# Both products of a feed forward by seven products of half-sized blocks in place of eight

## The reference

```python
h2 = rms_norm(x, norm2[l])
x = x + jnp.square(jax.nn.relu(h2 @ w_up[l])) @ w_down[l]
return rms_norm(x, final_norm)
```

## Time and profile before

| | |
|---|---|
| median of 3 runs | 1938.89 us (1938.49 to 1940.59) |
| the profiled execution | 1938.64 us; span 1936.6 us |
| busy: PE, DVE, ACT, POOL | 1904.5, 968.0, 778.3, 92.8 us |
| granted clock of TensorE, mean | 1.000 |
| chain that ended last | PE 89%, DVE 6%, ACT 3%, issue 2% |
| moved by DMA | 129.29 MB |

### The profile page before, as it was taken

How to read it: one execution, slowest core, us unless ns; L and a number is a source line. 1 busy time by engine, 2 the same in 40 slices (tenths; PEclk the granted TensorE clock), 3 DMA queues, 4 the chain that set the end, 5 groups by cost and what they waited for, 6 DMA issues and landing times.

```text
span 1936.6 us, 23640 instructions
## 1 busy us (share of the span) xinstructions
PE 1904.5 (98%) x9297; PEld 1577.2 (81%) x9297; DVE 968.0 (50%) x2069; ACT 778.3 (40%) x1482; POOL 92.8 (5%) x165
## 2 busy tenths in 40 slices
PE   8999999999999999999999999999999999999998
PEld 6888888868888888887888888888888888888887
DVE  5788764546676666665321244433343433333234
ACT  5566333347777777776211132312030312212022
POOL 4111001100000000000000000000000000000000
PEclk9999999999999999999999999999999999999999
DMA  5410124322232212222321141212020211112002
GB/s 169 115 34 28 55 87 152 102 67 66 61 77 72 74 52 64 74 61 59 95 54 44 55 159 48 66 44 66 22 76 23 75 33 55 55 33 66 22 22 87
DMA packets 132479, 129.29 MB, mean 67 GB/s; under 512 B 7233, under 2 KB 112265, under 8 KB 132370
## 3 DMA queue, kind: packets, MB, share of 16 engines
q1 hardware_dynamic: 126482, 115.18, 19.7%
q0 software_dynamic: 5888, 12.62, 2.9%
...
## 4 chain that ended last, share of the span: by engine, by line
PE 89%; DVE 6%; ACT 3%; issue 2%; DMA 0%; POOL 0%; DVEq 0%; POOLq 0%; SPq 0%; ACTq 0%
PE b L86 85%; PE b L89 4%; DVE Wf L108 1%; DVE Wr L97 1%; ACT Wf L94 1%; DVE Xr L97 1%; ACT Wf L93 1%; DVE Wf L97 1%; ACT Wr L93 1%; DVE ring L97 1%; ACT Xr L93 0%; DVE Yf L105 0%; DVE Wf L101 0%; DVE Yr L105 0%; ACT ring L93 0%
## 5 line engine op out<-in xcount | busy, mean ns | idle before, releaser
L86 PE MATMUL b<-Yr,ring 128*128 128x512 f32 x1920 | 507.9, 400 | 1.1 <-DVE Xr L97 1.1
L86 PE MATMUL b<-Xr,ring 128*128 128x512 f32 x1872 | 452.7, 393 | 3.3 <-DVE Xr L97 1.5
L86 PEld LDWEIGHTS b<-Xr,ring 128*128 128x128 f32 x1872 | 345.6, 189 | 70.9 <-issue 4.2
L86 PEld LDWEIGHTS b<-Yr,ring 128*128 128x128 f32 x1920 | 340.1, 189 | 56.0 <-DVE Xr L97 1.5
L86 PE MATMUL b<-Xr,Yr 128*128 128x512 f32 x1104 | 254.0, 390 | 0.0
L86 PEld LDWEIGHTS b<-Xr,Yr 128*128 128x128 f32 x1104 | 206.8, 188 | 42.8
L86 PE MATMUL b<-Yr 128*128 128x512 f32 (+2 forms) x1040 | 236.1, 375 | 0.0
L86 PEld LDWEIGHTS b<-Yr 128*128 128x128 f32 x1040 | 190.7, 188 | 38.1
L97 DVE TENSOR_TENSOR Wf<-Wf,b 128x512 f32<-128x512 f32 x144 | 92.6, 684 | 237.7 <-PE b L86 237.7
L93 ACT ACTIVATE Wf<-b 128x512 f32<-128x512 f32 (+3 forms) x215 | 106.2, 494 | 229.1 <-PE b L86 225.5
L94 ACT ACTIVATE Wf<-Wf,st 128x640 f32<-128x640 f32 (+3 forms) x192 | 125.2, 652 | 162.1 <-DVE st L112 58.8
...
## 6 DMA issues: line engine op xcount, KB each, us to landing
stage<-in_w_in_dram SPq DMA_DIRECT2D x58, 512.0 KB, 4.0
stage<-in_w_up_dram SPq DMA_DIRECT2D x32, 512.0 KB, 4.0
stage<-in_w_down_dram SPq DMA_DIRECT2D x32, 512.0 KB, 3.5
stage<-in_w_out_dram SPq DMA_DIRECT2D x16, 512.0 KB, 3.5
...
Yf<-in_x_dram SPq DMA_DIRECT2D x8, 512.0 KB, 6.4
Wf<-in_x_dram SPq DMA_DIRECT2D x8, 512.0 KB, 4.4
scratch_x<-Wf SPq DMA_DIRECT2D x8, 512.0 KB, 2.7
```

The costliest lines, as they stand in the source:

```text
L86: return self.send(lambda e: e.matmul(o, w, a, start=start, stop=stop))
```

## The change

Both products are made by the seven-product scheme (Winograd's form of Strassen's). With a 2 x 2 split of each operand, blocks of the weights or of the hidden values are combined into S1 to S4, blocks of the other operand into T1 to T4, and seven products P1 to P7 of half-sized blocks take the place of eight; their sums give the four quarters of the result.

**Up phase.** All of the up product comes first. A pair i of 16 has two groups of 128 columns of `w_up`. For each pair VectorE forms S1, S2 (`s12f`) and S4, S3 (`s43f`); ScalarE and VectorE split these and the plain blocks into high and low parts (`a`, `s12`, `s43`, `a22`). T1, T2, T3 of the activations are made tile by tile from the transposes of tiles 4 to 7 (`tile`, `lows`), T4 later in one piece (`T4f`, `T4`). A product is 12 matmuls. P6, P7 and P4 continue to sum on P1's bank and P3 on P5's (`matmul_onto`, L90 in the changed kernel); copies of the sums between are `r1`, `z5`, `u2`. ScalarE makes relu and square of the four results, VectorE their combinations (`US`, `U4`), and seven kinds of block are written to a new tensor `u_d` in HBM. The table UP_ORDER gives the order in every queue.

**Down phase.** 28 steps n: 4 chunks c of 1024 hidden channels by 7 products. A step is 48 matmuls. A share of `u_d` is loaded for each; ScalarE and VectorE split it (S) and the weights' block (T); GpSimd forms T1 to T4 of the weights. VectorE adds the banks to seven sums in SBUF (in the first chunk ScalarE copies four of them). In the last chunk the seven sums are combined, by GpSimd in pieces of 128 x 2048 and by VectorE, and the final norm follows. The rows of x wait in HBM during the up phase.

```diff
@@ tensor_program @@
-             (7, 3): turn_h3(5)})
+             (7, 3): turn_h3(5), (7, 6): turn_h3(6)})
-    for c in range(8):
-...
+    def seventh(kind, i, room, k0, acts, b, fresh):
+        w = room.rearrange("p (l k c) -> p l k c", l=2, c=P)
+        for k in range(4):
+            for n, (lw, la) in enumerate(((0, 0), (0, 1), (1, 0))):
+                last = k == 3 and n == 2
+                if fresh:
+                    sent = pe.matmul(m.banks[b], w[:, lw, k0 + k, :], acts[:, k, la, :], k == 0 and n == 0, last)
+                else:
+                    sent = pe.matmul_onto(m.banks[b], w[:, lw, k0 + k, :], acts[:, k, la, :], last)
+        sent.then_inc(m.p_dense, (kind, i))
+    for kind, i in UP_ORDER:
+        p, q, r = P_BANKS[i % 3], Q_BANKS[i % 2], R_BANKS[i % 2]
+        if kind == "tile" and i == 7:
+            turn_rows("f", 7, m.ht3[1], TURN_BANKS)
+        elif kind == "P1":
+            pe.wait_ge(*at["low", "a", i])
+            pe.wait_ge(*at["ht", "f", 3, 1])
+            pe.wait_ge(*at[freed[p]])
+            seventh("P1", i, m.room_a[i % 2], 0, m.B11, p, True)
+...
+        elif kind == "P4":
+            pe.wait_ge(*at["low", "a22", i])
+            pe.wait_ge(*at["T4 low"])
+            pe.wait_ge(*at["C22", i])
+            seventh("P4", i, m.room_a22, 0, m.T4, p, False)
+            freed[p] = ("C21", i)
+    for n in range(28):
+        pe.wait_ge(*at["low S", n])
+        pe.wait_ge(*at["low T", n])
+        for t in range(4):
+            b = LAST_BANKS[(4 * n + t) % 8]
+            pe.wait_ge(*at[freed[b]])
+            for k in range(4):
+                for i, (ls, lt) in enumerate(((0, 0), (0, 1), (1, 0))):
+                    sent = pe.matmul(m.banks[b], m.room_s[n % 2][:, k, ls, block(t)], m.room_t[n % 2][:, k, lt, :],
+                                     k == 0 and i == 0, k == 3 and i == 2)
+            sent.then_inc(m.p_dense, ("back", n, t))
+            note.bank["back", n, t] = b
@@ the tables of the order @@
+    out = [("post", 7), ("tile", 6), ("row", 7), ("P1", 0), ("lows", 6), ("P2", 0), ("C11", 0), ("P1", 1), ("tile", 7),
+           ("lows", 7), ("P2", 1), ("P5", 0), ("s43f", 0), ("s43", 0), ("P6", 0), ("a22", 0), ("P3", 0), ("s12f", 1),
+           ("s12", 1), ("P7", 0), ("US", 0), ("C11", 1), ("P5", 1), ("s43f", 1), ("T4f", 0), ("P6", 1), ("a", 2),
+           ("P1", 2), ("s43", 1), ("P3", 1), ("T4", 0), ("P4", 0), ("U4", 0), ("s12f", 2), ("a22", 1), ("P7", 1),
+           ("s12", 2)]
+    for i in range(2, PAIRS):
+        if i > 2:
+            out += [("P1", i), ("P7", i - 1)]
+        out += [("P5", i), ("s43f", i), ("US", i - 1), ("P2", i), ("C11", i), ("s43", i), ("P4", i - 1), ("U4", i - 1)]
+        if i < PAIRS - 1:
+            out += [("a", i + 1), ("P6", i), ("s12f", i + 1), ("P3", i), ("s12", i + 1), ("a22", i)]
+        else:
+            out += [("P6", i), ("P3", i), ("a22", i), ("prep", 0), ("P7", i), ("US", i), ("P4", i), ("U4", i)]
+    return out
+...
+DOWN_ORDER = ("P1", "P5", "P2", "P3", "P6", "P7", "P4")
+STORED = ("A11", "A12", "A22", "S1", "S2", "S3", "S4")
+SHARE_OF = {"P1": "A11", "P2": "A12", "P3": "S4", "P4": "A22", "P5": "S1", "P6": "S2", "P7": "S3"}
+P_BANKS, Q_BANKS, R_BANKS = (0, 4, 5), (1, 7), (2, 3)
+LAST_BANKS = (6, 4, 5, 1, 7, 2, 3, 0)
@@ scalar_program @@
+    def weights_high(part, i):
+        if part == "a":
+            room, src, free = m.room_a[i % 2][:, 0:1024], slot_a, ("P2", i - 2) if i > 1 else ("nat", "out2", 7, 0)
+            act.wait_ge(*at["up loaded", i, 0])
+            act.wait_ge(*at["merged sum", 7, 1])
+...
+        act.wait_ge(*at[free])
+        act.activation(room, src, FN.Copy).then_inc(m.a_w, ("high", part, i))
+    def relu_square(name, i, out, src, made, free):
+        act.wait_ge(*at[made])
+        act.wait_ge(*at[free])
+        act.activation(out, src, FN.Relu).then_inc(m.a_ev, (f"{name} relu" if src is out else "C21", i))
+        act.wait_ge(*at[f"{name} relu" if src is out else "C21", i])
+        act.activation(out, out, FN.Square).then_inc(m.a_ev, (name, i))
+    def prep_high(n):
+        c, kind = n // 7, DOWN_ORDER[n % 7]
+        act.wait_ge(*at["share loaded", n])
+        act.wait_ge(*at[("back", n - 2, 3) if n > 1 else ("P3", PAIRS - 1) if n else ("P5", PAIRS - 1)])
+        act.activation(m.room_s[n % 2][:, :, 0, :], m.sf[n % 2], FN.Copy).then_inc(m.a_w, ("high S", n))
+        act.wait_ge(*at[back_ready(c, kind)])
+        act.wait_ge(*at[("back", n - 2, 3) if n > 1 else ("P6", PAIRS - 1) if n else ("P2", PAIRS - 1)])
+        act.activation(m.room_t[n % 2][:, :, 0, :], back_source(m, c, kind), FN.Copy).then_inc(m.a_w, ("high T", n))
@@ vector_program @@
+    def tile(t):
+        b0, b1 = [m.banks[note.bank["turned", "f", t, x]].rearrange("p (k t) -> p k t", k=4) for x in range(2)]
+...
+        dve.wait_ge(*at["turned", "f", t, 0])
+        dve.wait_ge(*at["ht", "f", t - 4, 0])
+        dve.tensor_tensor(t1, b0, high, ALU.subtract).then_inc(m.v_lo, ("T1 first", t))
+        dve.wait_ge(*at["T1 first", t])
+        dve.tensor_tensor(t1, t1, low, ALU.subtract).then_inc(m.v_lo, ("T1 full", t))
+...
+    post_f(5)
+    weights_low("a", 0)
+    mean_square("f", 3, 5)
+    row_h3(5)
+    tile(4)
+    lows(4)
+    post_f(6)
+    mean_square("f", 3, 6)
+...
+        elif kind == "s43f":
+            sums_43(i)
+        elif kind == "T4f":
+            hi, lo = [m.plain["T4"][:, :, part, :] for part in range(2)]
+            dve.wait_ge(*at["T2 low", 7])
+            dve.wait_ge(*at["nat", "out2", 7, 7])
+            dve.tensor_tensor(hi, f32(m.B21[:, :, 0, :]), f32(m.T2[:, :, 0, :]), ALU.subtract)
+            dve.tensor_tensor(lo, f32(m.B21[:, :, 1, :]), f32(m.T2[:, :, 1, :]), ALU.subtract).then_inc(m.v_lo, "T4 parts")
+            dve.wait_ge(*at["T4 parts"])
+            dve.tensor_tensor(lo, hi, lo, ALU.add).then_inc(m.v_lo, "T4 full")
+        elif kind == "T4":
+            dve.wait_ge(*at["T4 high"])
+            dve.tensor_tensor(m.T4[:, :, 1, :], m.plain["T4"][:, :, 1, :], f32(m.T4[:, :, 0, :]), ALU.subtract).then_inc(
+...
+    for n in range(28):
+        added(n, 0)
+        if n + 1 < 28:
+            prep_low(n + 1, "S")
+        added(n, 1)
+        if n + 1 < 28:
+            prep_low(n + 1, "T")
+        if n == 22:
+            dve.wait_ge(*at["added", 21, 3])
+            dve.tensor_tensor(m.sum6, m.sum6, m.sum1, ALU.add).then_inc(m.v_ev, "P6 with P1")
+        if n == 27:
+            row_out(4)
+        added(n, 2)
+        if n == 27:
+            row_out(5)
+        added(n, 3)
+    row_out(6)
@@ gpsimd_program @@
+    for c in range(4):
+        b11, b12 = m.half0[c % 2][:, :, 0, :], m.half0[c % 2][:, :, 1, :]
+        b21, b22 = m.half1[:, :, 0, :], m.half1[:, :, 1, :]
+        pool.wait_ge(*at["half0", c])
+        if c:
+            pool.wait_ge(*at["T4 of", c - 1])
+            pool.wait_ge(*at["low T", 7 * c - 3])
+        else:
+            pool.wait_ge(*at["P6", PAIRS - 2])
+        pool.tensor_tensor(m.t12, b12, b11, ALU.subtract).then_inc(m.g_b, ("T1 of", c))
+        if c == 3:
+            pool.wait_ge(*at["added", 21, 3])
+            pool.wait_ge(*at["added", 16, 3])
+            pool.tensor_tensor(m.c11, m.c11, m.sum1, ALU.add).then_inc(m.g_b, "C11 with P1")
+        pool.wait_ge(*at["half1", c])
+        pool.wait_ge(*at["T1 of", c])
+        pool.tensor_tensor(b12, b22, b12, ALU.subtract).then_inc(m.g_b, ("T3 of", c))
+        pool.wait_ge(*at["low T", 7 * c + 1])
+        pool.tensor_tensor(m.t12, b22, m.t12, ALU.subtract).then_inc(m.g_b, ("T2 of", c))
+        if c == 3:
+            pool.wait_ge(*at["added", 22, 3])
+            pool.wait_ge(*at["added", 17, 3])
+            pool.tensor_tensor(m.c12, m.c12, m.sum5, ALU.add).then_inc(m.g_b, "C12 with P5")
+        pool.wait_ge(*at["low T", 7 * c + 2])
+        pool.wait_ge(*at["T2 of", c])
+        pool.tensor_tensor(b21, b21, m.t12, ALU.subtract).then_inc(m.g_b, ("T4 of", c))
+    for t in range(4, 8):
+        pool.wait_ge(*at["x2 again", t])
+    pool.tensor_tensor(m.c22, m.c22, m.sum5, ALU.add).then_inc(m.g_b, "C22 with P5")
@@ sync_program @@
+    def keep(name, i, src, made):
+        n = STORED.index(name)
+        sp.wait_ge(*at[made])
+        sp.dma_start(m.u_d[i // 4, n, :, i % 4, :], src).then_inc(m.d_u[n], ("kept", name, i), 16)
+    def share(n):
+        c, name = n // 7, SHARE_OF[DOWN_ORDER[n % 7]]
+        sp.wait_ge(*at["kept", name, 4 * c + 3])
+        sp.dma_start(m.sf[n % 2], m.u_d[c, STORED.index(name)]).then_inc(m.d_sf[n % 2], ("share loaded", n), 16)
+    def down_tiles(c, second):
+        dst = m.half1 if second else m.half0[c % 2]
+        for j in range(4):
+            r0 = c * 1024 + second * 512 + j * P
+            sp.dma_start(dst[:, j], m.w_down_2[0][r0:r0 + P, :].rearrange("p (h c) -> p h c", h=2)).then_inc(
+...
+    for n in range(28):
+        c = n // 7
+        sp.wait_ge(*at["low S", n])
+        if n + 2 < 28:
+            share(n + 2)
```

(49 more changed lines are left out.)

592 lines of the change are left out of this document (413 added, 179 removed).

## The result

The change makes the kernel 1.3% slower: 1963.76 us (median of four, 1960.89 to 1967.36) against 1938.76, a ratio of 1.0128 (95% interval 1.011 to 1.0146). The sign is the one forecast and the time lies in the range, but the loss is 25 us where 11.7 was predicted.

A forecast was written before the change was run, and what follows sets the result against it. Matmuls on TensorE were taken to set the time, the other engines having room. Losses of 98.8 us less the saving of 87.1 gave +11.7 on 1938.64, so 1950.3 us, with a range from 1905 to 1975.

The forecast's parts named there:

- The sign: The whole kernel: slower, with chance 0.56, against 0.32 for faster and 0.12 for the same.
- The saving: Up and down products: 384 fewer matmuls at 226.7 ns each, -87.1 us.
- The entry: Start of the up phase: TensorE waits for ScalarE and VectorE up to P7(1), steady from pair 3, +45.4 us.
- the first 18.9: Start of the up phase: TensorE loses 18.9 us before P5(0), because VectorE's chain ends only at 1263.0.
- The exit: From up to down: `prep` parts ahead of C22(15) delay P4(15) by 7.35, GpSimd's T3 adds 4.45; +11.8 us.
- the share: Start of the down phase: the third share queues behind the rows of x, +1 us.
- The last chunk: Down steps 22, 23, 25, 26: losses of 3.6, 10.7, 2.0, 7.5, mostly VectorE and GpSimd taking turns; +23.8 us.
- chunks 1 and 2: Down phase: VectorE collides with GpSimd's T3, one of two counted at 2.4 us.
- the tail: After TensorE's last matmul: 13.8 us in place of 6.6, from a longer chain of quarter rows; +7.2 us.
- Rival A: VectorE and GpSimd share rather than take turns, or miss each other: about 1918, 1900 with half the entry; chance 0.30.
- the restarts of the clock: After TensorE's largest gaps: slow matmuls, four of six gaps counted at 1.8 us each, +7.2, bounds 0 and 10.8.
- Rival C: Steady pairs: VectorE's chains exceed the slack of 0.8 us, so waits recur in each pair; about 1976, chance 0.14.

The follow-up runs named there:

- e2: The changed kernel with the high and low part of the first up weights moved behind the lows of tile 4 on ScalarE and VectorE: 1954.39 us.
- e3: The changed kernel with pair 2's weights `a` and pair 1's s43 parts ahead of T4f, and P4(0) behind P7(1) and pair 2's sums: 1946.89 us.
- e9: The changed kernel with six stops of TensorE, 0.81 to 7.99 us, after P7 of pairs 3, 5, 7, 9, 11, 12: 1997.06 us.

## Why the prediction was right and wrong

**The saving** is there: 384 matmuls less at 226.4 ns in the pairs.

**The entry** (45.4) came out as 36.9 of waits: 8.1, 2.9, 6.2 and 5.4 where 8.8, 3.1, 6.5 and 5.8 stood, and 1.9 where 2.3 did. In place of the first 18.9 there are 12.4, but the slow groups of that stretch hold 5.7 more, and P5(0) started at 1261.4 where VectorE's chain was said to end at 1263.0. e2 and e3 confirm the causes, the two instructions at the head of VectorE's queue.

**The exit** (11.8, and 1 for the share) is 8.7 and 4.9. The sum is near, the working was not: GpSimd's T3 missed C22 (it ran at 1597.28, 4.55 us, beside `US`); instead a store landed 11.1 us after its issue, and the share behind the rows of x was worth 4.9. I had given those transfers 1 us from the loads of the earlier trace rows, which were measured in a quiet stretch (43 GB/s in the earlier trace rows, 260 here).

**The last chunk** (23.8) is 22.2: 3.4, 10.0, 1.8, 7.0 where 3.6, 10.7, 2.0 and 7.5 stood; chunks 1 and 2 gave 3.2 for 2.4, the tail 6.1 for 7.2. Rival A, sharing in place of taking turns, is refuted by the 6.70 and 6.66 above (an even split would at most double 2.28), and with half the entry it comes to 1896, not 1900. The Trainium skill ("SBUF — State Buffer", "SBUF: two separate sides") had this rule of an exclusive lock, and the trace agrees: 6.7 against 2.28 alone.

**The failed step is the restarts of the clock**: "I count four with 1.8 each", 7.2. They cost 26.2. The count was the larger mistake: I took four of the six largest gaps, while eleven groups of PE paid over 1 us here, and five of the six stops in e9, that of 1.85 us too. A product whose wait follows closely upon a restart (P3(1), 2.89) pays again. The price of one, 1.8 from the earlier trace rows, was somewhat low: 1.5 to 2.6 in e9, 1.4 to 2.6 here. Eleven at 1.8 are 19.8; the other 6.4 are the higher price and slow neighbours. The rule of the Trainium skill ("TensorE: Matmul & The Clock Gate", "HAM oscillation — how this bites in real kernels"), that every such gap pays, was put beside the sum at 3.6 more. The trace agrees for its six gaps, each followed by a group 2.0 to 2.6 us slow; e9 shows that gaps shorter than these six pay as well. With 26.2 in place of 7.2, and the other terms at their forecast, the sum would have been +30.7; with the waits as measured it is +21.1 of 22.6. That the total came no further off is luck: the waits were forecast at 84.4 us in all and came to 75.9, and these 8.5 hid nearly half of the 19.0 by which the restarts were too cheap.

**Rival C** did not happen: there is no wait in any pair from 3 to 14. How much of the forecast slack of 0.8 us was left is not read.
